# First feed-forward phase of a one-core decoder trunk: the input in four loads, its squares on ScalarE, their sums on VectorE

## Chip, cores and metric

One of the eight cores of a Trainium2 chip runs the whole program. The metric is the time of one execution on the device, in microseconds, as a median over runs. Names of engines in the rows: PE is TensorE (PEld its weight loads), DVE is VectorE, ACT is ScalarE, POOL is GpSimd, SP is the engine that issues most of the loads. A "q" behind a name (SPq, POOLq) is the engine's own instruction queue.

## What is computed

```python
for i in range(DEPTH):                       # DEPTH = 2, so six phases
    h = h + 0.5 * swiglu(rms_norm(h, norm_ff1[i]), ffn1_gate[i], ffn1_up[i], ffn1_down[i])
    hn = rms_norm(h, norm_mix[i])
    ...                                      # i = 0: SSD and RG-LRU mixer, i = 1: differential attention
    h = h + 0.5 * swiglu(rms_norm(h, norm_ff2[i]), ffn2_gate[i], ffn2_up[i], ffn2_down[i])
return rms_norm(h, final_norm)

def rms_norm(x, w, eps=1e-6):
    return x * lax.rsqrt(jnp.mean(x * x, axis=-1, keepdims=True) + eps) * w
def swiglu(x, w_gate, w_up, w_down):
    return (jax.nn.silu(x @ w_gate) * (x @ w_up)) @ w_down
```

x is 256 tokens by 1024 features in float32, and the hidden width is 2816. The work of the change lies wholly in the first `rms_norm` and the first products of the first `swiglu`.

## The kernel before

The residual stream `h` lies in SBUF with features on the partitions: eight tiles of 128 features by 256 tokens. The program goes through six phases: feed-forward (ffn), hybrid mixer (hyb), ffn, ffn, attention (att), ffn. Every matrix is read once from memory in blocks of 128 output columns, 512 KB each (704 KB for the down matrices), into a ring of four slots (`raw`).

**Split products.** To multiply float32 on TensorE, each operand is cut into a high part and the rest. ScalarE copies a block to `whi` (`split_hi`, L168), VectorE subtracts to get `wlo` (`split_lo`, L175). The residual tiles are cut alike into `xn[:, d, 0]` (ScalarE, `residual_hi`, L263, with the norm's weight as scale) and `xn[:, d, 1]` (VectorE, `residual_lo`, L271). `multiply_wide` (L196) then issues two matmuls for each of the eight feature tiles: one of 512 columns (L206) and one of 256 (L207). I call these two a step; a block has eight steps.

**Pairs.** In a ffn phase a gate block and an up block make a pair. There are 22 pairs, then eight pairs of down blocks. Pair 0 is made of blocks 0 and 1, pair 1 of blocks 2 and 3, and so on. Even pairs use PSUM banks 2 and 3, odd ones 0 and 1. So before pair 2 TensorE must know that pair 0 was read out (`s_gu`, L382), which VectorE signals in `merge` (L442).

**The norm.** The factor 1/rms of a token is not applied to x, but to the products: `normalize` (L450) multiplies by `rb`. Here is how `rb` comes about. GpSimd squares the eight tiles and adds them up one by one (`residual_square`, L281; lines 287, 290, 294). TensorE sums over the partitions with a matrix of ones (`token_sums`, L300), ScalarE takes the root (`token_rms`, L314), VectorE the reciprocal (`token_scale`, L320). In every phase the sums stand on TensorE between its first and its second pair (L378).

**Orders.** Every engine runs its own list of instructions in the order in which the functions below issue them. Nothing is scheduled; a wait at the head of a list holds all that stands behind it. SP issues the loads of the start in this order: the vectors `vec`, x tiles 0 to 3, block 0, x tiles 4 to 7, blocks 1, 2, 3, the constants `con`, `heads` (L1595, L1596, L339 to L350). From block 4 on each load waits until its ring slot was split. GpSimd, when it has done the squares of the first phase, clears a part of `arena` and issues the small loads of the hybrid phase (`hyb_weights`, L622) and of `lamin` (L1644).

VectorE's list of the first phase is written in `ffn_vector`, L473 to L485, and ScalarE's in L411 to L420:

```python
for g in range(2):
    before[g]()
    if p0 + g == 0:
        split_lo(dve, 0, 0, DT)
        for d in range(1, DT):
            residual_lo(dve, 0, d)
        split_lo(dve, 1, 1, DT)
    else:
        convert_lo(dve, p0 + g, DT)
token_scale(dve, n)
```

Of the kernel before, what the change touches and what calls it, by code (L numbers as in the profile page):

```python
# [21 lines left out]
D, T, FF = 1024, 256, 2816  # L22
DT, FT = D // P, FF // P
# [50 lines left out]
def trunk(nc, a, out, phases=PHASES):  # L74
    ctx = ExitStack()
    with ctx:
# [35 lines left out]
        s_const = sem("s_const")  # L112
        s_x = [sem(f"s_x{i}") for i in range(2)]
        s_eps = sem("s_eps")
# [8 lines left out]
        s_sq = sem("s_sq")  # L123
        s_acc = sem("s_acc")
        s_stat = sem("s_stat")
        s_rms = sem("s_rms")
# [37 lines left out]
        def load_x(sp, i):  # L164
            tiles = slice(i * DT // 2, (i + 1) * DT // 2)
            sp.dma_start(h[:, tiles, :], a["xT"].rearrange("(d p) t -> p d t", p=P)[:, tiles, :]).then_inc(s_x[i], 16)
# [89 lines left out]
        def fresh(eng, n, d):  # L256

            if n == 0:
                eng.wait_ge(s_x[d // (DT // 2)], 16)
            else:  # L260
                eng.wait_ge(s_h, DT * (n - 1) + d + 1)
# [9 lines left out]
        def residual_lo(dve, n, d):  # L271
            if n == len(phases):
                return
            if n:
# [4 lines left out]
                                     xn[:, d, 0, :].bitcast(F32), ALU.mult, ALU.subtract).then_inc(s_xlo, 1)  # L279

        def residual_square(pool, n, d):  # L281

            fresh(pool, n, d)
            if d == 0:
                if n:
                    pool.wait_ge(s_stat, n)
                pool.tensor_tensor(sumsq[:], h[:, d, :], h[:, d, :], ALU.mult).then_inc(s_acc, 1)  # L287
                return
            pool.wait_ge(s_acc, DT * n + d)
            pool.tensor_tensor(sq[:], h[:, d, :], h[:, d, :], ALU.mult).then_inc(s_sq, 1)  # L290
            if n == len(phases) and d == DT - 1:
                return
            pool.wait_ge(s_sq, (DT - 1) * n + d)
            pool.tensor_tensor(sumsq[:], sumsq[:], sq[:], ALU.add).then_inc(s_acc, 1)
# [5 lines left out]
        def token_sums(pe, n):  # L300

            end = n == len(phases)
            pe.wait_ge(s_acc, DT * (n + 1) - end)
            if n:
                pe.wait_ge(s_rms, n)
            else:
                pe.wait_ge(s_const, 32)
            mm = pe.matmul(sums_bank(n), ones, sumsq[:], start=True, stop=not end)
            if end:
                pe.wait_ge(s_sq, (DT - 1) * (n + 1))  # L310
                mm = pe.matmul(sums_bank(n), ones, sq[:], start=False, stop=True)
            mm.then_inc(s_stat, 1)
# [12 lines left out]
        def add_residual(dve, n, d, acc, scale):  # L325

            dve.wait_ge(s_acc, DT * n + d + 1)
            dve.scalar_tensor_tensor(h[:, d, :], acc, scale, h[:, d, :], ALU.mult, ALU.add).then_inc(s_h, 1)
# [6 lines left out]
        def ffn_sync(sp, n, i):  # L335
# [3 lines left out]
            def gate_up(it, ring_full):  # L339
                for s in range(RING):  # L340
                    if s == 1 and not ring_full:
                        load_x(sp, 1)
                    c = it * (2 * P) + (s // 2) * P
                    load(sp, it * RING + (b0 + s), s,
                         (gate, up)[s % 2][:, bass.ds(c, P)].rearrange("(k p) m -> p k m", p=P), DT, ring_full)
# [13 lines left out]
        def ffn_tensor(pe, n, i):  # L359
# [17 lines left out]
            gate_up(p0, 0, lambda t: pe.wait_ge(s_xlo, DT * n + t + 1), lambda: read_out(pe, p0 - 1))  # L377
            token_sums(pe, n)  # L378
            gate_up(p0 + 1, 1)
            with pe.Fori(1, FT // 2) as it:  # L380
                for g in range(2):
                    pe.wait_ge(s_gu, it * 2 + (hb + g - 1))  # L382
                    gate_up(it * 2 + (p0 + g), g)
# [8 lines left out]
        def ffn_scalar(act, n, i, before):  # L392
# [18 lines left out]
# [3 lines that stand above are left out]
                    split_hi(act, 0, 0, DT, 0)  # L414
                    for d in range(1, DT):
                        residual_hi(act, 0, d)
                    split_hi(act, 1, 1, DT, 0)
                else:
                    convert_hi(act, p0 + g, DT, n > 0)
            token_rms(act, n)  # L420
            for it in range(1, FT // 2):
# [17 lines left out]
        def ffn_vector(dve, n, i, before):  # L439
# [33 lines left out]
            for g in range(2):  # L473
# [6 lines left out]
                else:  # L480
                    convert_lo(dve, p0 + g, DT)
            token_scale(dve, n)
            if n == 0:
# [17 lines left out]
        def down_out(dve, n, d):  # L501
            p = first[n] + FT + d
            dve.wait_ge(s_blk, 2 * p + 2)
            dve.wait_ge(s_acc, DT * n + d + 1)
            acc = wide(0, d % 2)
# [1087 lines left out]
        @block.sync  # L1593
        def _(sp):
            sp.dma_start(vec[:], a["vec"]).then_inc(s_vec, 16)  # L1595
            load_x(sp, 0)  # L1596
            for n, (kind, i) in enumerate(phases):
# [13 lines left out]
        @block.scalar  # L1611
        def _(act):
            act.wait_ge(s_vec, 16)
            act.wait_ge(s_eps, 1)
            before = [lambda: residual_hi(act, 0, 0), lambda: None]
# [21 lines left out]
        def _(pool):  # L1637
            for n in range(len(phases) + 1):
                for d in range(DT):
                    residual_square(pool, n, d)  # L1640
# [69 lines left out]
```

## Time and profile before

| | |
|---|---|
| runs | 1110.90, 1111.77, 1115.74 us |
| median | 1111.77 us |
| span of the profiled execution | 1110.4 us |
| TensorE matmul busy | 1068.7 us, 96% of the span |
| VectorE busy | 827.0 us, 74% |
| ScalarE busy | 600.6 us, 54% |
| GpSimd busy | 169.8 us, 15% |
| read from memory | 184.78 MB, 167 GB/s over the span |

The profiled execution has no time of its own beside its span in what was left; the span lies 1.4 us below the median and 0.5 us below the fastest run. The span is counted from the first instruction to the last. The busy time of matmuls is modelled, so 96% does not say that the engine is at its peak; it says that it is seldom without work.

### The profile page before, as it was taken

Reading aid. Unit: us, or ns where it says so; the run is one execution under the profiler, and the core shown is the slowest. Engines: PE = TensorE matmul, PEld = TensorE weight load, DVE = VectorE, ACT = ScalarE, POOL = GpSimd, SP = SyncE. Lnnn points to the kernel's source line nnn. Section 1 sums busy time; section 2 is a strip of 40 time slices with the busy share of each in tenths; the row PEclk is TensorE's granted clock in tenths of the full one; section 3 lists DMA queues with packets and bytes.
Section 4 is the critical chain, followed back from the end, with each engine's and each line's share of the span. In section 5 each row is a group of like instructions: output and inputs, shape, how many; then the busy total and the mean of one; then the engine's idle time right before and its main releaser. Section 6 shows DMA issues by size and latency. Waiting matters only on the chain.

```text
span 1110.4 us, 18481 instructions
## 1 busy us (share of the span) xinstructions
PE 1068.7 (96%) x6671; PEld 947.7 (85%) x6671; DVE 827.0 (74%) x1150; ACT 600.6 (54%) x915; POOL 169.8 (15%) x156
## 2 busy tenths in 40 slices
PE   6999999999999999999999999999999899999996
PEld 4888888897888998888888888888988888888885
DVE  6878765799887868887656888765679778788753
ACT  5555543565866546555535555544535745555442
POOL 7000011223443330000021000012111041000011
PEclk9999999998998999999999999999999999999999
DMA  8766675454443566667665666676544336666761
GB/s 241 199 193 190 197 208 163 139 145 114 122 115 107 153 181 180 190 195 206 179 191 147 195 191 189 188 205 176 167 137 119 110 92 189 192 191 198 201 187 38
DMA packets 364307, 186.51 MB, mean 168 GB/s; under 512 B 5456, under 2 KB 363984, under 8 KB 364256
## 3 DMA queue, kind: packets, MB, share of 16 engines
q1 hardware_dynamic: 364000, 185.26, 58.9%
q0 software_dynamic: 256, 0.59, 0.2%
q8 instruction: 29, 0.48, 0.2%
q14 instruction: 22, 0.18, 0.0%
HBM read 184.78 MB, written 1.05 MB: 167 GB/s over the span
## 4 chain that ended last, share of the span: by engine, by line
PE 83%; DVE 11%; issue 3%; ACT 2%; POOL 0%; DMA 0%; DVEq 0%; ACTq 0%; SPq 0%; POOLq 0%
PE psum L206 44%; PE psum L207 22%; PE psum L190 5%; PE psum L191 4%; PE psum L192 4%; DVE wlo L178 3%; DVE xn L278 1%; ACT arena L1385 1%; DVE arena L913 1%; DVE small L1490 1%; PE psum L684 1%; DVE arena L1469 0%; PE psum L718 0%; DVE arena L1512 0%; POOL wlo L178 0%
## 5 line engine op out<-in xcount | busy, mean ns | idle before, releaser
L206 PE MATMUL psum<-xn,whi 128*128 128x512 f32 x1408 | 496.2, 397 | 11.2 <-DVE wlo L178 10.3
L178 DVE TENSOR_TENSOR wlo<-raw,whi 128x1024 fp32r<-128x1024 f32 (+1 forms) x317 | 419.4, 1342 | 62.4 <-ACT whi L173 61.5
L207 PE MATMUL psum<-xn,wlo 128*128 128x256 f32 x1408 | 393.9, 280 | 0.0
L173 ACT ACTIVATE whi<-raw 128x1024 fp32r<-128x1024 f32 (+1 forms) x322 | 352.7, 1112 | 46.9 <-PE psum L192 45.1
L206 PEld LDWEIGHTS psum<-xn,whi 128*128 128x128 f32 x1408 | 265.3, 188 | 75.7 <-DVE wlo L178 10.6
L207 PEld LDWEIGHTS psum<-xn,wlo 128*128 128x128 f32 x1408 | 266.7, 189 | 0.1
L206 PE MATMUL psum<-hid,whi 128*128 128x512 f32 x704 | 246.9, 396 | 4.7 <-issue 4.7
L207 PE MATMUL psum<-hid,wlo 128*128 128x256 f32 x704 | 196.9, 280 | 0.0
L206 PEld LDWEIGHTS psum<-hid,whi 128*128 128x128 f32 x704 | 132.0, 188 | 37.1 <-issue 5.9
L190 PE MATMUL psum<-xn,whi 128*128 128x256 f32 x480 | 142.6, 297 | 1.9 <-DVE wlo L178 1.9
L191 PE MATMUL psum<-xn,whi 128*128 128x256 f32 x480 | 138.0, 287 | 0.0
L192 PE MATMUL psum<-xn,wlo 128*128 128x256 f32 x480 | 137.9, 287 | 0.0
L207 PEld LDWEIGHTS psum<-hid,wlo 128*128 128x128 f32 x704 | 132.8, 189 | 0.0
L190 PEld LDWEIGHTS psum<-xn,whi 128*128 128x128 f32 x480 | 94.4, 197 | 6.4 <-issue 5.6
L191 PEld LDWEIGHTS psum<-xn,whi 128*128 128x128 f32 x480 | 94.3, 197 | 1.5 <-issue 1.4
L404 ACT ACTIVATE arena<-arena 128x256 f32<-128x256 f32 x88 | 36.8, 418 | 107.8 <-DVE arena L452 107.8
L192 PEld LDWEIGHTS psum<-xn,wlo 128*128 128x128 f32 x480 | 94.2, 196 | 0.0
L287 POOL TENSOR_TENSOR sumsq<-h 128x256 f32<-128x256 f32 x7 | 5.2, 742 | 578.8 <-DVE h L508 514.8
L269 ACT ACTIVATE xn<-h,vec 128x256 fp32r<-128x256 f32 x48 | 23.3, 505 | 123.0 <-DVE h L508 106.6
L408 ACT ACTIVATE hid<-arena 128x256 fp32r<-128x256 f32 x88 | 36.8, 418 | 88.7 <-DVE arena L457 88.7
L462 DVE TENSOR_TENSOR hid<-arena,hid 128x256 f32 (+1 forms) x88 | 37.4, 425 | 58.5 <-ACT hid L408 58.5
L290 POOL TENSOR_TENSOR sq<-h 128x256 f32<-128x256 f32 x49 | 37.0, 755 | 195.6 <-DVE h L508 172.5
(196 smaller groups left out, 1151.5 us busy)
## 6 DMA issues: line engine op xcount, KB each, us to landing
raw<-in_ffn_gate SPq DMA_DIRECT2D x88, 512.0 KB, 3.8
raw<-in_ffn_up SPq DMA_DIRECT2D x88, 512.0 KB, 4.0
raw<-in_ffn_down SPq DMA_DIRECT2D x64, 704.0 KB, 4.8
raw<-in_hyb_w_in SPq DMA_DIRECT2D x36, 512.0 KB, 3.8
raw<-in_dif_w_qkv SPq DMA_DIRECT2D x24, 512.0 KB, 4.5
raw<-in_hyb_w_out SPq DMA_DIRECT2D x16, 512.0 KB, 4.6
raw<-in_dif_w_o SPq DMA_DIRECT2D x8, 512.0 KB, 4.3
h<-in_xT SPq DMA_DIRECT2D x2, 512.0 KB, 5.4
```

What stands on the lines that cost most here:

```text
L173: act.activation(whi[:, s, 0:k * P], raw[:, s, 0:k * P], ACT.Copy).then_inc(s_whi, 1)
L178: dve.tensor_tensor(wlo[:, s, 0:k * P], raw[:, s, 0:k * P], whi[:, s, 0:k * P].bitcast(F32), ALU.subtract).then_inc(s_wlo, 1)
L190: pe.matmul(acc, w_hi, x[:, t, 0, :], start=start and j == 0, stop=False)
L191: pe.matmul(acc, w_hi, x[:, t, 1, :], start=False, stop=False)
L192: mm = pe.matmul(acc, w_lo, x[:, t, 0, :], start=False, stop=stop and j == k - 1)
L206: pe.matmul(acc, w_hi, x[:, t, :, :], start=start and j == 0, stop=False)
L207: mm = pe.matmul(acc[:, T:2 * T], w_lo, x[:, t, 0, :], start=False, stop=stop and j == k - 1)
L269: act.activation(xn[:, d, 0, :], h[:, d, :], ACT.Copy, scale=vec[:, w:w + 1]).then_inc(s_xhi, 1)
L290: pool.tensor_tensor(sq[:], h[:, d, :], h[:, d, :], ALU.mult).then_inc(s_sq, 1)
L404: act.activation(act_g[:, g, :], gu[:, g, 0, :], ACT.Silu).then_inc(s_silu, 1)
L408: act.activation(hid[:, bass.ds(j, 1), 0, :].rearrange("p a t -> p (a t)"), hu[:, g, :], ACT.Copy).then_inc(s_hhi, 1)
L462: dve.tensor_tensor(v[:, 1, :], hu[:, g, :], v[:, 0, :].bitcast(F32), ALU.subtract).then_inc(s_hlo, 1)
```

## The change

- x comes in four loads of two tiles each, with a semaphore each. The first is issued ahead of `vec`, the second behind it, the third and fourth ahead of blocks 1 and 2.
- ScalarE runs a small Sqrt on `eps` as its first instruction, ahead of its wait for `vec`. Its table load then stands there.
- In the first phase GpSimd does no squares and sums. ScalarE squares the tiles two at a time (`input_squares`), behind its first four weight splits. VectorE adds them up in three halving additions (`input_sums`), behind its first four weight splits and ahead of `token_scale`.
- TensorE's `token_sums` of the first phase stands behind pair 1, not between pairs 0 and 1.
- GpSimd's list begins with `hyb_weights` and the load of `lamin`.
- `down_out` of the first phase no longer waits for GpSimd's sums, and the counts of `s_acc` and `s_sq` are one phase lower.

```diff
         def load_x(sp, i):
-            tiles = slice(i * DT // 2, (i + 1) * DT // 2)
+            tiles = slice(2 * i, 2 * i + 2)
             sp.dma_start(h[:, tiles, :], a["xT"].rearrange("(d p) t -> p d t", p=P)[:, tiles, :]).then_inc(s_x[i], 16)
...
             if n == 0:
-                eng.wait_ge(s_x[d // (DT // 2)], 16)
+                eng.wait_ge(s_x[d // 2], 16)
...
+        xsq = arena[:, 4096:4096 + DT * T].rearrange("p (d t) -> p d t", d=DT)
+
+        def input_squares(act):
+            for d in range(0, DT, 2):
+                act.activation(xsq[:, d:d + 2, :], h[:, d:d + 2, :], ACT.Square).then_inc(s_xsq, 1)
+
+        def input_sums(dve):
+            dve.wait_ge(s_xsq, DT // 2 + 1)
+            dve.tensor_tensor(xsq[:, 0:4, :], xsq[:, 0:4, :], xsq[:, 4:8, :], ALU.add).then_inc(s_xadd, 1)
+            dve.wait_ge(s_xadd, 1)
+            dve.tensor_tensor(xsq[:, 0:2, :], xsq[:, 0:2, :], xsq[:, 2:4, :], ALU.add).then_inc(s_xadd, 1)
+            dve.wait_ge(s_xadd, 2)
+            dve.tensor_tensor(sumsq[:], xsq[:, 0, :], xsq[:, 1, :], ALU.add).then_inc(s_xadd, 1)
...
         def token_sums(pe, n):
...
-            pe.wait_ge(s_acc, DT * (n + 1) - end)
             if n:
+                pe.wait_ge(s_acc, DT * (squares_before(n) + 1) - end)
                 pe.wait_ge(s_rms, n)
             else:
+                pe.wait_ge(s_xadd, 3)
                 pe.wait_ge(s_const, 32)
...
                 for s in range(RING):
-                    if s == 1 and not ring_full:
-                        load_x(sp, 1)
+                    if not ring_full and s in (1, 2):
+                        load_x(sp, s + 1)
...
             gate_up(p0, 0, lambda t: pe.wait_ge(s_xlo, DT * n + t + 1), lambda: read_out(pe, p0 - 1))
-            token_sums(pe, n)
+            if n:
+                token_sums(pe, n)
             gate_up(p0 + 1, 1)
+            if n == 0:
+                token_sums(pe, n)
...
+            if n == 0:
+                input_squares(act)
             token_rms(act, n)
...
+            if n == 0:
+                input_sums(dve)
             token_scale(dve, n)
...
         def _(sp):
+            load_x(sp, 0)
             sp.dma_start(vec[:], a["vec"]).then_inc(s_vec, 16)
-            load_x(sp, 0)
+            load_x(sp, 1)
...
         def _(act):
+            act.wait_ge(s_eps, 1)
+            act.activation(small[:, 0:1], eps[:, 0:1], ACT.Sqrt).then_inc(s_xsq, 1)
             act.wait_ge(s_vec, 16)
-            act.wait_ge(s_eps, 1)
...
             for n in range(len(phases) + 1):
-                for d in range(DT):
+                for d in range(DT) if n else ():
                     residual_square(pool, n, d)
```

The lists of three engines show where things went. TensorE, before, at the end of pair 0 (`sumsq` by `con` is the matmul with ones):

```order
L206 MATMUL psum<-xn,whi 128x512
L207 MATMUL psum<-xn,wlo 128x256
L308 MATMUL psum<-sumsq,con 128x256 [waits s_const,s_acc]
L206 MATMUL psum<-xn,whi 128x512 [waits s_wlo]
L207 MATMUL psum<-xn,wlo 128x256
```

TensorE, changed, at the end of pair 1:

```order
L208 MATMUL psum<-xn,whi 128x512
L209 MATMUL psum<-xn,wlo 128x256
L327 MATMUL psum<-sumsq,con 128x256 [waits s_const,s_xadd]
L402 UNCONDITIONAL_BRANCH
L402 ISA
L202 ISA [waits s_gu]
L208 MATMUL psum<-xn,whi 128x512 [waits s_wlo]
```

The sums moved past the sixteen steps of pair 1, and now stand right ahead of the wait for the read-out of pair 0 (`s_gu`), with which pair 2 begins.

VectorE, changed, from its first weight split on:

```order
L180 TENSOR_TENSOR wlo<-raw,whi 128x1024 [waits s_whi]
L280 SCALAR_TENSOR_TENSOR xn<-h,vec,xn 128x256 [waits s_xhi] x7
L180 TENSOR_TENSOR wlo<-raw,whi 128x1024 [waits s_whi] x3
L291 TENSOR_TENSOR arena<-arena 128x1024 [waits s_xsq]
L293 TENSOR_TENSOR arena<-arena 128x512 [waits s_xadd]
L295 TENSOR_TENSOR sumsq<-arena 128x256 [waits s_xadd]
L341 RECIPROCAL rb<-rms 128x256 [waits s_rms]
L180 TENSOR_TENSOR wlo<-raw,whi 128x1024 [waits s_whi,s_rb]
L472 TENSOR_TENSOR arena<-psum,arena 128x512 [waits s_cor,s_blk]
```

The three additions are new. The reciprocal, the split of block 4 and the read-out of pair 0 (`arena<-psum,arena`, which signals `s_gu`) keep their order behind them.

GpSimd, changed, from its first instruction of the program on:

```order
L651 MEMSET arena 128x2048
L656 DMA arena<-in_lru_w_ra 64x8x64 [waits s_zero]
L656 DMA arena<-in_lru_w_ra 64x8x64
L656 DMA arena<-in_lru_w_ix 64x8x64 x2
L657 DMA arena<-in_hyb_w_in 128x8x16
L1673 DMA small<-in_lam 64x4
```

Before, fifteen squares and additions stood ahead of these rows, the first of them waiting for x; now nothing does.

## Rows read from the trace of the kernel before

**Rows 1.** The page, busy time: engine, us, share of the span, instructions.
```profile
PE 1068.7 (96%) x6671; PEld 947.7 (85%) x6671; DVE 827.0 (74%) x1150; ACT 600.6 (54%) x915; POOL 169.8 (15%) x156
```

**Rows 2.** Chain that ended last, 0 to 28 us: start us, us, what.
```profile
5.14 1.28 ACT L269
6.95 1.07 ACT whi L173
9.27 5.74 DVE xn L278 x7
15.01 1.56 DVE wlo L178
16.61 0.50 PE psum L206
17.92 0.43 PE psum L206
18.35 0.21 PE psum L207
21.23 0.43 PE psum L308 x2
21.66 0.23 PE psum L206
27.21 0.23 PE psum L206
```

**Rows 3.** Timeline of SP: start us, us, queue, line, operation, tile.
```profile
1.68 0.50 SPq L162 DMA_DIRECT2D raw<-in_ffn_gate  x1
2.22 0.58 SPq L166 DMA_DIRECT2D h<-in_xT  x1
```

**Rows 4.** DMA issues at 1.68, 2.22, 2.84, 3.74, 6.21: size, us to landing.
```profile
raw<-in_ffn_gate SPq DMA_DIRECT2D x1, 512.0 KB, 5.3
h<-in_xT SPq DMA_DIRECT2D x1, 512.0 KB, 6.9
raw<-in_ffn_up SPq DMA_DIRECT2D x1, 512.0 KB, 8.1
raw<-in_ffn_gate SPq DMA_DIRECT2D x1, 512.0 KB, 9.0
raw<-in_ffn_up SPq DMA_DIRECT2D x1, 512.0 KB, 8.3
```

**Rows 5.** Stretches: us, busy of PE, PEld, DVE, ACT, POOL, granted clock, DMA share, GB/s.
```profile
5.00:10.00 5.00, 0.68 (x2) 0.50 (x2) 2.46 (x3) 4.84 (x9) 4.29 (x6) 1.00 1.08 311
15.00:20.00 5.00, 4.00 (x13) 3.23 (x14) 4.78 (x4) 1.84 (x2) 4.70 (x4) 0.70 0.62 175
20.00:21.00 1.00, 1.00 (x6) 0.84 (x5) 0.00 (x0) 0.00 (x0) 1.00 (x2) 0.78 0.68 175
```

**Rows 6.** VectorE's cutting of x: one line's durations in ns over the program.
```profile
L278 DVE SCALAR_TENSOR_TENSOR xn<-h,vec,xn x48: 471/485/962, 7.1 to 916.1; 128x256 fp32r<-128x256 f32 x48
```

**Rows 7.** Timeline, 14.9 to 26 us: start us, us, engine, line, operation, tiles.
```profile
14.93 4.86 DVE L178 TENSOR_TENSOR wlo<-raw,whi 128x1024 fp32r<-128x1024 f32 x3
...
23.99 1.23 DVE L178 TENSOR_TENSOR wlo<-raw,whi 128x1024 fp32r<-128x1024 f32 x1
25.13 0.69 DVE L448 TENSOR_TENSOR arena<-psum,arena 128x512 f32<-128x512 f32 x1
...
20.32 1.80 POOL L624 MEMSET arena<- 128x2048 f32 x1
```

**Rows 8.** DMA queues, 22 to 32 us: packets, MB, share of 16 engines.
```profile
q0 software_dynamic: 256, 0.59, 22.1%
```

**Rows 9.** Stretches around a stall of TensorE, columns as in rows 5.
```profile
346.00:348.00 2.00, 0.00 (x0) 0.00 (x0) 2.00 (x2) 0.95 (x1) 1.90 (x1) 1.00 0.54 146
356.00:358.00 2.00, 2.00 (x12) 2.00 (x11) 2.00 (x5) 2.00 (x7) 0.00 (x0) 0.50 0.01 2
```

More of the change, by code:

```diff
@@ L112, in trunk @@
         s_const = sem("s_const")
-        s_x = [sem(f"s_x{i}") for i in range(2)]
+        s_x = [sem(f"s_x{i}") for i in range(4)]
         s_eps = sem("s_eps")
@@ L124, in trunk @@
         s_acc = sem("s_acc")
+        s_xsq = sem("s_xsq")
+        s_xadd = sem("s_xadd")
         s_stat = sem("s_stat")
@@ L279, in residual_lo, with squares_before @@
                                      xn[:, d, 0, :].bitcast(F32), ALU.mult, ALU.subtract).then_inc(s_xlo, 1)
+        xsq = arena[:, 4096:4096 + DT * T].rearrange("p (d t) -> p d t", d=DT)
[9 more added lines that the diff above has]
+            dve.tensor_tensor(sumsq[:], xsq[:, 0, :], xsq[:, 1, :], ALU.add).then_inc(s_xadd, 1)
+        def squares_before(n):
+            return n - 1
         def residual_square(pool, n, d):
@@ L284, in residual_square @@
             if d == 0:
-                if n:
-                    pool.wait_ge(s_stat, n)
+                pool.wait_ge(s_stat, n)
                 pool.tensor_tensor(sumsq[:], h[:, d, :], h[:, d, :], ALU.mult).then_inc(s_acc, 1)
                 return
-            pool.wait_ge(s_acc, DT * n + d)
+            pool.wait_ge(s_acc, DT * squares_before(n) + d)
             pool.tensor_tensor(sq[:], h[:, d, :], h[:, d, :], ALU.mult).then_inc(s_sq, 1)
@@ L292, in residual_square @@
                 return
-            pool.wait_ge(s_sq, (DT - 1) * n + d)
+            pool.wait_ge(s_sq, (DT - 1) * squares_before(n) + d)
             pool.tensor_tensor(sumsq[:], sumsq[:], sq[:], ALU.add).then_inc(s_acc, 1)
@@ L309, in token_sums @@
             if end:
-                pe.wait_ge(s_sq, (DT - 1) * (n + 1))
+                pe.wait_ge(s_sq, (DT - 1) * (squares_before(n) + 1))
                 mm = pe.matmul(sums_bank(n), ones, sq[:], start=False, stop=True)
@@ L325, in add_residual @@
         def add_residual(dve, n, d, acc, scale):
-            dve.wait_ge(s_acc, DT * n + d + 1)
+            dve.wait_ge(s_acc, DT * squares_before(n) + d + 1)
             dve.scalar_tensor_tensor(h[:, d, :], acc, scale, h[:, d, :], ALU.mult, ALU.add).then_inc(s_h, 1)
@@ L503, in down_out @@
             dve.wait_ge(s_blk, 2 * p + 2)
-            dve.wait_ge(s_acc, DT * n + d + 1)
+            if n:
+                dve.wait_ge(s_acc, DT * squares_before(n) + d + 1)
             acc = wide(0, d % 2)
```

## Prediction

> **What bounds the kernel now.** I read the page first. Matmuls keep TensorE busy for 1068.7 of 1110.4 us [rows 1], so a change counts only by what it does to TensorE's line of work. The edits all lie in the first phase, so the next view is the chain of waits of the first 28 us [rows 2]. Until 16.61 us TensorE waits for others; from there on the chain runs on TensorE alone, through pairs 0 and 1 and into pair 2, whose first matmul stands at 27.21. Between 21.66 and 27.21 lie 16 steps, so a step takes 0.347 us at the full clock and a pair 5.55. The granted clock is 0.70 in the mean from 15 to 20 us and 0.78 from 20 to 21 [rows 5]: with two levels, 1 and 0.5, that makes 3.0 and 0.4 us at the lower one (1.2 GHz), 3.4 in all, after a stretch in which TensorE often waited. There a step takes 0.43 + 0.21 = 0.64 us [rows 2]. So a microsecond at the low clock gives away 1 - 0.347/0.64 = 0.46 us.
>
> My measure is the start of pair 2: 27.21 us before. What comes behind it is the same work, on which TensorE is busy without a gap, so the end moves by as much as that start does.
>
> What holds the front? Block 0 is issued at 1.68 and lands 5.3 us later [rows 3, 4], at 6.98, and ScalarE's first split begins at 6.95 [rows 2]. x tiles 4 to 7, issued at 2.22, land at 9.1 [rows 3, 4]. Blocks 1, 2 and 3, issued at 2.84, 3.74 and 6.21, land at 10.9, 12.7 and 14.5 [rows 4], a block each 1.8 us. The DMA share is 1.08 from 5 to 10 us at 311 GB/s [rows 5]: the queue is full. Behind the first weight split VectorE cuts the other seven x tiles in 5.74 us, 0.82 each [rows 2], while the same instruction has a median of 0.485 us over the program [rows 6]. GpSimd is busy 4.29 of those 5 us [rows 5]; I take its squares to be what slows VectorE. The three weight splits behind take 1.62 each [rows 7], against 1.23 for the split at 23.99, when GpSimd does no more squares [rows 7].
>
> **Part 1, x in quarters and the early table load.** The table load of 1.28 us at 5.14 [rows 2] goes to the idle start. It gains nothing: the split behind it needs block 0, which lands at 6.98, and the bytes ahead of block 0 are the same (vec and half of x). The first quarter of x comes earlier, but TensorE needs block 0 beside it. The other table load that goes, ahead of the root, ran while ScalarE was idle: nothing either. The last quarter of x now stands behind block 1. Half of x plus two blocks landed by 9.1 and 10.9, so I put the third quarter at 8.0, block 1 at 10.0, the fourth quarter at 10.9, blocks 2 and 3 as before.
>
> **Part 2, GpSimd leaves.** VectorE's cut is 0.485, its split 1.2. Without any other effect: cuts of tiles 1 to 5 from 9.3 to 11.7, tiles 6 and 7 to 12.7. ScalarE gets to block 1 when it has copied tile 7, at about 11.8, and takes 1.07 [rows 2]; VectorE then splits to 14.1. TensorE could begin block 1 at 14.1 where it began at 16.61: a gain of 2.5 us.
>
> **Part 3, what GpSimd does instead.** Its list now begins with the clearing, 1.80 us [rows 7], so its five loads are issued from about 3 us on, into the full queue. They cost the 16 DMA engines 22.1% of 10 us = 2.2 us [rows 8], for 0.59 MB; at 300 GB/s the bytes alone are 2.0. Lower end: nothing, if they slip in between. Upper end: 2.2 on every landing behind them. I take 2.1 for the fourth quarter and all blocks behind, and 0.9 for block 0 (it lands at 7.9), since the share of 1.08 leaves no room. Then the fourth quarter lands at 13.0; ScalarE copies tiles 6 and 7 to 13.9 and block 1 to 15.0, VectorE splits to 16.2. Block 1 begins at 16.2, a gain of 0.4.
>
> The Trainium skill (DMA: Bandwidth & Descriptors, on queues, rings and completion order) says that each DMA engine takes turns between its queues packet by packet; that speaks against this part, since the later queue gets its turn at once. The same page (anatomy of one DMA) prices the moving at bytes over 436 GB/s, by which the delay would be 1.35 us and the total 0.7 lower; the trace's 22.1% is nearer to the case.
>
> **Part 4, squares and sums.** Four squares of 512 columns on ScalarE, each half a split of 1024 (1.07, so 0.53) [rows 2]: 2.1 us, behind block 3's split. With block 3 landing at 16.6 that is 17.7 to 19.8. On VectorE the additions are 1.2, 0.7 and 0.4 (a read-out of 512 columns is 0.69 [rows 7]): 2.3 us, to 22.1. TensorE does pair 1 until 24.5 or later, so the sums are in time and cost nothing by themselves. Their cover is pair 1.
>
> **Part 5, the sums behind pair 1: the new wait.** Before, from the matmul with ones (21.23 [rows 2]) through the root, the reciprocal and the split of block 4 to the end of the read-out of pair 0 (25.13 + 0.69 = 25.82 [rows 7]) took 4.6 us, and TensorE did pair 1 meanwhile. Now pair 1 is done when this chain begins, and TensorE's next instruction waits for exactly that read-out. The whole 4.6 us, matmul included, lies on TensorE's path. Bounds: none of it is hidden by what stands in the lists, so the lower end is 4.6 less nothing; the upper adds the clock.
>
> **The clock after the stall.** From 346 to 348 us TensorE stood still, and at 356 to 358, busy again, its clock was 0.50 [rows 9]; in the first phase it fell after less idle time than that [rows 5]. So I count a low clock after this stall too: a loss of 3.4 x 0.46 = 1.5 us as in rows 5, or at most that of the 10 us from 348 to 358, 4.6; I take 1.5, since there the wide matmuls of this same phase followed. Below, it is nothing if the clock holds. For pairs 0 and 1 I take the full clock, as the gap ahead of block 1 shrinks to about 1 us between busy work.
>
> **The sum.** Block 1 begins at 16.2; 24 steps of 0.347 are 8.3; slow first steps 0.3; chain 4.6. That gives 29.4 for the start of pair 2, plus 1.5 of clock: 30.9 against 27.2, so 3.7 us more. The span goes to 1110.4 + 3.7 = 1114.1. The span lies 1.4 below the median of the runs, so the median to expect is 1111.8 + 3.7 = **1115.5 us**.
>
> **Rivals.**
> - *The five loads don't delay.* For it: from 22 to 32 us they ran beside block loads, which TensorE did not feel. Against: the queue was not full by then. Block 1 begins at 14.1: 2.1 us less, 1113.4.
> - *The front gain outweighs the stall.* This needs the loads harmless and a clock that stays full after the stall: 14.1 + 8.3 + 4.6 = 27.0, and with no low stretch at all 1111.6; a quicker first block (x is there at 4 us, if block 0 is too) could bring one more, 1110.6. Against it is the clock in rows 9.
> - *Slower by more than 0.5%: the clock falls twice.* The place is pairs 0 and 1 as well as pair 2. If the gap ahead of block 1 costs 3.4 us at the low level as it did before, 1.5 more, and the fall after the stall lasts twice the 3.4 us counted, 1.5 more again: 1115.5 + 3.0 = 1118.5. It decides from about 4 us of low clock beyond those counted (1.8/0.46). For it: the 10 us of rows 9; against: dense wide matmuls follow here.
> - *The change doesn't do what it says:* it was not GpSimd that slowed VectorE. Then the cuts and splits stay at 0.82 and 1.6. The landings hide most of it; the last two cuts and one split add about 1.1: 1116.6.
>
> **Chances.** Forecast 0.45; loads harmless 0.18; gain outweighs 0.12; clock twice 0.17; not GpSimd 0.05; the rest 0.03 for things that I don't see. A measurement of this kernel tells about 0.5%, 5.6 us, from no change. All cases but the clock falling twice lie within that. So slower by more than 0.5% gets 0.17, faster 0.02, within 0.81. The range has to leave out no more than 0.2: it reaches down to 1111.0, into the case of the gain, and up to 1118.8.
>
> **What would show it right or wrong.** In the profile of the changed kernel: the first matmul of pair 2 waits 4 to 5 us for VectorE's read-out (not for a weight split), and its start lies at 29 to 31. GpSimd's loads are issued at 3 to 7 us, and blocks 2 and 3 land at about 14.9 and 16.6; if they land at 12.7 and 14.5, part 3 is wrong. VectorE's seven cuts last 0.5 each; if they last 0.8, part 2 is. The granted clock is 0.50 behind the stall; if it is 1.00 there, 1.5 us go. If pair 2 begins without a gap, part 5 is wrong and the prediction with it; a change of more than 5 us behind 30 us would mean that I looked at the wrong place.

## The result, and the profile after

The kernel with the change takes 1123.97 us (median of 4 runs, 1122.67 to 1126.98), the kernel before 1113.76 beside it (4 runs, 1110.9 to 1117.32). The ratio is 1.0100, with an interval of 1.0073 to 1.0126: about 1% slower. The profiled execution took 1123.17 us, its span is 1121.3, 10.9 more than before. I had forecast 1115.5 and at most 1118.8, so the prediction was wrong. Its direction was right, its size was a third of the real one. The result fell into the case "slower by more than 0.5%", to which I had given 0.17.

The page of the kernel after, busy time per engine, beside [rows 1]:

```profile
PE 1071.6 (96%) x6671; PEld 949.1 (85%) x6671; DVE 827.8 (74%) x1153; ACT 602.4 (54%) x919; POOL 154.3 (14%) x141
```

GpSimd lost 15 us of work, and the others have what they had. So work did not grow much; TensorE waits. The chain of waits of the kernel after, 0 to 40 us (start us, us, what), answers to [rows 2]:

```profile
4.02 11.91 DMA h<-in_xT
15.95 0.91 ACT xn L271 x2
16.86 0.96 ACT whi L175
17.84 1.24 DVE wlo L180
19.12 0.79 PE psum L208
20.13 0.43 PE psum L208
...
22.57 0.23 PE psum L208
29.16 0.45 PE psum L327 x2
29.63 0.48 ACT rms L337
30.14 1.76 DVE rb L341
31.96 1.11 issue
33.07 0.69 DVE arena L472
33.88 0.79 PE psum L208
...
39.37 0.28 PE psum L208
```

Read it in three parts. The front hangs on a DMA: the last quarter of x, issued at 4.02, lands 11.91 us later. (From here on I read a landing off the start of the ScalarE instruction that takes the tiles up, 15.95 here.) Block 1 begins at 19.12, where it began at 16.61. From 29.16 on the chain leaves TensorE: matmul with ones, root, reciprocal, split of block 4, read-out of pair 0 (L472), and only then pair 2, at 33.88. Pair 2 stood at 27.21 before [rows 2]: 6.7 us later. TensorE's waits in the first 50 us (line, what it waited for: us in total, times, longest) give the size of each wait:

```profile
PE psum L208 <- DVE wlo L180: 10.8, 2, 10.4
PE psum L208 <- DVE arena L472: 4.3, 1, 4.3
PE psum L208 <- DVE xn L280: 2.4, 1, 2.4
```

The stretches of the kernel after, columns as in [rows 5]:

```profile
5.00:10.00 5.00, 0.00 (x0) 0.00 (x0) 0.90 (x1) 1.99 (x4) 2.16 (x4) 1.00 1.12 258
10.00:15.00 5.00, 4.21 (x12) 3.22 (x12) 2.31 (x6) 1.07 (x3) 0.00 (x0) 1.00 1.12 195
...
25.00:30.00 5.00, 4.59 (x27) 3.70 (x25) 0.04 (x1) 0.37 (x1) 0.00 (x0) 1.00 0.32 83
30.00:35.00 5.00, 1.11 (x3) 1.02 (x4) 4.79 (x5) 4.18 (x6) 0.00 (x0) 0.75 0.07 20
35.00:40.00 5.00, 5.00 (x19) 4.25 (x19) 3.96 (x7) 2.84 (x5) 0.00 (x0) 0.56 0.69 196
```

From 10 to 15 us the DMA engines are as busy as before (1.12) but move only 195 GB/s. The same stretch of the kernel before:

```profile
10.00:15.00 5.00, 4.75 (x14) 2.67 (x12) 5.00 (x8) 3.50 (x6) 4.33 (x7) 1.00 1.14 322
```

They are busy with something that carries few bytes. From 30 to 35 TensorE works 1.11 us in 5. The granted clock is 0.75 in the mean of that stretch and 0.56 in the next: the lower level of 1.2 GHz until 39.4, where the step drops from 0.64 to 0.35 us (39.37 in the chain). Whose DMA is it? GpSimd's timeline (start us, us, ...) shows its loads now going out from 2.85 us:

```profile
0.74 1.80 POOL L651 MEMSET arena<- 128x2048 f32 x1 [0.29 <-POOLq L1732]
2.85 1.54 POOL L656 DMA_DIRECT2D arena<-in_lru_w_ra  x2 [0.30 <-POOL arena L651]
4.38 1.36 POOL L656 DMA_DIRECT2D arena<-in_lru_w_ix  x2
5.73 0.90 POOL L657 DMA_DIRECT2D arena<-in_hyb_w_in  x1
```

and VectorE's timeline shows that its own part went as hoped:

```profile
10.24 2.06 DVE L280 SCALAR_TENSOR_TENSOR xn<-h,vec,xn 128x256 fp32r<-128x256 f32 x5
16.49 0.88 DVE L280 SCALAR_TENSOR_TENSOR xn<-h,vec,xn 128x256 fp32r<-128x256 f32 x2 [4.19 <-ACT xn L271]
17.84 2.36 DVE L180 TENSOR_TENSOR wlo<-raw,whi 128x1024 fp32r<-128x1024 f32 x2 [0.47 <-ACT whi L175]
...
22.63 1.23 DVE L291 TENSOR_TENSOR arena<-arena 128x1024 f32<-128x1024 f32 x1 [0.86 <-ACT arena L287]
...
30.14 1.75 DVE L341 RECIPROCAL rb<-rms 128x256 f32<-128x256 f32 x1 [5.09 <-ACT rms L337]
```

Five cuts in 2.06 us are 0.41 each, half of the 0.82 before. GpSimd has issued its last load by 7.2 us and does nothing beside them. But 4.19 us stand ahead of the last two, spent waiting for x, and 5.09 ahead of the reciprocal, spent waiting for the matmul with ones.

### The profile page after: what moved, and what is told of

It is laid out like the page before. It is cut to its first block, busy times and chain, and to the rows that moved or that the text cites. A ratio compares the mean times of both kernels' runs of the same rounds, so it can differ in the third digit from the quotient of the medians.

```text
span 1121.3 us, 18460 instructions
## 1 busy us (share of the span) xinstructions
PE 1071.6 (96%) x6671; PEld 949.1 (85%) x6671; DVE 827.8 (74%) x1153; ACT 602.4 (54%) x919; POOL 154.3 (14%) x141
## 4 chain that ended last, share of the span: by engine, by line
PE 81%; DVE 12%; issue 3%; ACT 2%; DMA 1%; SPq 0%; DVEq 0%; ACTq 0%
PE psum L208 44%; PE psum L209 22%; PE psum L192 4%; PE psum L193 4%; PE psum L194 4%; DVE wlo L180 4%; DVE arena L940 2%; DMA h<-in_xT 1%; ACT arena L1412 1%; DVE small L1517 1%; DVE xn L280 1%; DVE arena L1496 0%; DVE rb L341 0%; PE psum L745 0%; PE psum L711 0%
## 5 line engine op out<-in xcount | busy, mean ns | idle before, releaser
L175 ACT ACTIVATE whi<-raw 128x1024 fp32r<-128x1024 f32 (+1 forms) x322 | 352.3, 1112 | 43.8 <-PE psum L194 39.2
L472 DVE TENSOR_TENSOR arena<-psum,arena 128x512 f32<-128x512 f32 x88 | 60.3, 685 | 4.4 <-ACT arena L421 3.9
```

The lines of the kernel that those rows point to most:

```text
L175: act.activation(whi[:, s, 0:k * P], raw[:, s, 0:k * P], ACT.Copy).then_inc(s_whi, 1)
L472: dve.tensor_tensor(gu[:, g, :, :], wide_parts(g)[0], cor[:, g, :, :], ALU.add).then_inc(s_gu, 1)
```

## The experiments

Two things are on trial: GpSimd's small loads in the full queue (front), and the sums behind pair 1 (stall and clock). Each expectation names its own theories A, B and C. The kernel before was run beside each group; its median there was 1113.53, 1114.39 and 1113.18 us (21, 19 and 23 runs, 1107.5 to 1119.8 in all).

**late_small_loads**: the kernel after, GpSimd's loads as late as before.

```diff
+                        pool.wait_ge(s_stat, 1)
                         hyb_weights(pool)
```

> The changed kernel, but GpSimd waits for the first phase's column sums (matmul with ones) before it clears the arena and issues its five small loads. Theory A (the small loads, issued at 2.9 to 6.6 us into a full queue, hold up x's last quarter and block 1): the last quarter, issued at about 4 us, lands near 11 instead of 15.9, block 1 begins near 14 instead of 19.1, pair 2 near 28 to 29 instead of 33.9, and the time falls by 5 to 6 us to about 1118. Theory B (the last quarter is late because it now stands behind block 1 in SP's list, whoever else loads): it lands at 14 or later, pair 2 begins at 32 or later, the time moves by less than 2 us. Both: the wait of 4.3 us at the head of pair 2 stays.

1115.47 us (6 runs), ratio 1.0028 (1.0006 to 1.0049): 8.5 us of median less than the kernel after, from one wait. In the trace the fourth quarter lands at 11.8, where it landed at 15.9. VectorE's timeline of this kernel:

```profile
10.75 2.86 DVE L280 SCALAR_TENSOR_TENSOR xn<-h,vec,xn 128x256 fp32r<-128x256 f32 x7
13.69 2.36 DVE L180 TENSOR_TENSOR wlo<-raw,whi 128x1024 fp32r<-128x1024 f32 x2
```

Seven cuts run through and block 1's split ends at 14.9. The matmul with ones stands at 23.88 (29.16 in the kernel after). The stall is still there in full, on TensorE's timeline:

```profile
28.61 0.79 PE L208 MATMUL psum<-xn,whi 128*128 128x512 f32 x1 [4.30 <-DVE arena L472]
...
29.41 0.63 PE L208 MATMUL psum<-xn,whi 128*128 128x512 f32 x1
30.05 0.63 PE L208 MATMUL psum<-xn,whi 128*128 128x512 f32 x1
```

Steps of 0.64 us behind it show the lower clock, until 31.7. With that clock loss (3.1 us at 0.46) pair 2 stands at 30.0, against 36.4 in the kernel after: 6.4 us come from the small loads.

Block 1 begins at 15.4, not at 14.9 when its split is ready, since TensorE is still at block 0: that block starts at 10.88, and its first steps last 0.64 us. small_loads_after_x, below, has block 1 at 15.4 too.

What the small loads do to the other queue is in the view of the DMA queues from 5 to 15 us (packets, MB, share of 16 engines), first of the kernel after, then of late_small_loads:

```profile
q1 hardware_dynamic: 2832, 1.67, 83.3%
q0 software_dynamic: 256, 0.59, 29.0%
```
```profile
q1 hardware_dynamic: 4929, 3.20, 111.4%
```

GpSimd's queue (q0) takes 2.9 us of the 16 engines' time for itself. SP's queue (q1) moves 1.67 MB in 8.3 us, 200 GB/s, where without the small loads it moves 287: its own packets take 2.5 us longer. Together that is 5.4 us of engine time for 0.59 MB. (The 256 packets of q0 are not the pieces of which I speak below: those, 3072, are counted from the access patterns of the program.)

**sums_between_pairs**: the kernel after, matmul with ones back between pairs 0 and 1.

```diff
-            if n:
-                token_sums(pe, n)
+            token_sums(pe, n)
             gate_up(p0 + 1, 1)
-            if n == 0:
-                token_sums(pe, n)
```

> The changed kernel, but with the matmul with ones back between pair 0 and pair 1. Theory A (its place behind pair 1 costs a stall of 4.6 us): TensorE now waits for the sums instead, from the end of pair 0 at about 22 to 25.1, then does pair 1, and the root, reciprocal and read-out are hidden; pair 2 begins at about 31 instead of 33.9 and the low clock behind it is shorter or gone: 3 to 5 us less, 1119 to 1121. Theory B (the stall only moves; what counts is when the sums are there): pair 2 begins at 33 or later and the time is the same within 1 us.

1116.48 us (10 runs), ratio 1.0037 (1.0018 to 1.0055), 7.5 less than the kernel after. The last quarter still lands at 16, and TensorE waits 1.0 us for the sums, which are ready at 25.1; but pair 2 starts at about 31.4 without a gap, and the clock holds:

```profile
25.00:30.00 5.00, 4.86 (x27) 4.29 (x28) 3.67 (x4) 4.10 (x5) 0.00 (x0) 1.00 0.33 82
30.00:35.00 5.00, 5.00 (x31) 4.35 (x30) 3.96 (x7) 3.22 (x6) 0.00 (x0) 1.00 0.72 202
```

31.4 against 27.2 is 4.2 us, and the ratio says 4.1. Undone alone, each of the two moves gives back 7 to 8.5 us of median; in the traces, start of pair 2 with its clock loss, it is 6.4 (loads) and 5.0 (order) of 9.2. The intervals of the two kernels overlap, so which of the two weighs more is not shown in time. Together they are more than the whole, so with both undone the absence of GpSimd's squares should be a gain (reordered, below, tests it).

**x_quarters_only**: the kernel before, with only x loaded in quarters in the new order.

```diff
...
-            sp.dma_start(vec[:], a["vec"]).then_inc(s_vec, 16)
             load_x(sp, 0)
+            sp.dma_start(vec[:], a["vec"]).then_inc(s_vec, 16)
+            load_x(sp, 1)
```

> The kernel before with nothing but the loads of x in quarters, in the order of the change (first quarter ahead of the vectors, last behind block 1). GpSimd still squares. Theory A (the order alone costs little): block 1 begins within 1 us of 16.6, pair 2 within 1 us of 27.2, the same time as before within 2 us. Theory B (the last quarter's place is costly): block 1 begins at 18 or later, pair 2 at 29 or later, 2 us or more slower.

1113.09 us (10 runs), ratio 0.9999 (0.9981 to 1.0016). The last quarter lands at 10.84, and block 1 begins at 17.3, 0.7 later than before; GpSimd still slows VectorE:

```profile
9.87 5.71 DVE L278 SCALAR_TENSOR_TENSOR xn<-h,vec,xn 128x256 fp32r<-128x256 f32 x7
15.50 4.02 DVE L178 TENSOR_TENSOR wlo<-raw,whi 128x1024 fp32r<-128x1024 f32 x3
```

0.82 a cut, as in [rows 2], with GpSimd's squares in place: it is they, and not the loads of x, that slow VectorE. The order of x costs nothing and brings nothing by itself in time.

**large_pieces**: late_small_loads plus the same bytes (0.59 MB) through GpSimd's queue at 1.28 us, but in pieces of 4608 bytes.

```diff
+                        pool.dma_start(arena[:, 7168:7168 + NCON], a["con"]).then_inc(s_big, 16)
                         pool.wait_ge(s_stat, 1)
+                        pool.wait_ge(s_big, 16)
                         hyb_weights(pool)
```

> As late_small_loads, but GpSimd issues at its very start one load of the same 0.59 MB in large pieces (4608 bytes each, the constants once more, into the part of the arena that is cleared later). Theory A (the count of small pieces of 64 and 256 bytes costs, not the bytes): the last quarter of x lands within 2.1 us of the kernel with late small loads, so at 13 or sooner, and pair 2 begins at most 2 us after it. Theory B (any 0.59 MB there costs the 5 us): it lands at 15 or later and pair 2 begins at 33 or later.

1113.5 us (one run, span 1111.7). Block 0 lands at 9.6, 1.1 later than without, the last quarter at 13.0, 1.2 later, the matmul with ones is at 25.54, 1.7 later. The same bytes in 2048 pieces of 256 bytes and 1024 of 64 made the last quarter 4.1 later. So it is not the bytes alone. Two things differ besides the size of the pieces, and no run parts them. The large load goes out at 1.28 us, 1.6 us ahead of the first small one; yet from 5 to 15 us this kernel moves 328 and 307 GB/s, the kernel after 258 and 195 at about the same share, so no such load is hidden there. And it is one load to 128 partitions, where the 256-byte pieces come in four loads to 64 partitions each.

**early_256_only and early_64_only**: the kernel after, with only one kind of small piece early. The first puts the wait ahead of the 64-byte load:

```diff
+            pool.wait_ge(s_stat, 1)
             pool.dma_start(wdt, a["hyb_w_in"][0][:, COL_DT:COL_DT + HEADS].rearrange("(k p) m -> p k m", p=P)
```

The second issues that load first, at 1.27 us, and waits ahead of everything else.

> The changed kernel, but of the five small loads only the four in pieces of 256 bytes (2048 pieces, 0.52 MB) are issued early; the one in pieces of 64 bytes and the last tiny one come behind the sums. Late small loads had the last quarter of x at 11.8, all early at 15.9. Theory A (cost by bytes): 0.52 of 0.59 MB, it lands at 15.5. Theory B (cost by pieces, 2048 of 3072): 14.5. Theory C (the 64-byte pieces are the dear ones): 13 or sooner.

> The changed kernel, but only the load in pieces of 64 bytes (1024 pieces, 0.07 MB) is issued early, as GpSimd's first instruction, the clearing and all others behind the sums. Theory A (bytes): the last quarter of x lands at 12.3 at most. Theory B (pieces, 1024 of 3072): about 13.2. Theory C (the 64-byte pieces are the dear ones): 14 or later.

With the four 256-byte loads early (1123.63 us, one run) the last quarter lands at 15.2: 3.4 of the 4.1 us are theirs. With the 64-byte load alone, early, it lands at 11.3: no delay. Both are nearest to theory A, the cost by bytes (15.5, and 12.3 at most), not to the count of pieces (14.5 and 13.2). So between the two kinds of small pieces their number does not set the cost. SP's timeline shows a second trace of it. The issue of the constants takes 5.70 us in the kernel after, 4.75 with the 256-byte loads early, and 2.23 in late_small_loads (each row from its own kernel: after, early_256_only, late_small_loads):

```profile
10.18 5.70 SPq L368 DMA_DIRECT2D con<-in_con  x1
```
```profile
10.35 4.75 SPq L368 DMA_DIRECT2D con<-in_con  x1
```
```profile
9.50 2.23 SPq L368 DMA_DIRECT2D con<-in_con  x1
```

The time of early_64_only was not foreseen: 1123.97 us, span 1122.2, as slow as the kernel after, although its first 40 us are those of late_small_loads (sums at 24.08). Where those 10 us lie is told in the last section.

**small_loads_after_x**: the kernel after, the loads only once x is in (`pool.wait_ge(s_x[3], 16)` ahead of them).

> The changed kernel, but GpSimd waits for the last quarter of x before it clears and issues its small loads, so they come at about 14 us. Theory A: the last quarter lands near 11.8 and block 1 begins near 14.9 as with loads behind the sums; only blocks 3 and 4 and the constants, still in the queue then, land later, and pair 2 begins within 1 us of 28.5. Theory B (the loads cost the same wherever in the first 20 us they come): pair 2 begins at 31 or later.

1111.72 us (one run, span 1109.9). The last quarter lands at 11.4, the matmul with ones is at 23.87, pair 2 at 28.60 behind the stall of 4.3. GpSimd clears from 11.4 us on and issues from 13.5 to 17.8. The same pieces there, beside the end of block 3, the constants and the blocks from 4 on, delay nothing that TensorE waits for. The rate falls here too: 241 and 196 GB/s from 15 to 20 and 20 to 25 us, at shares of 1.12 and 1.17.

**old_small_loads_first**: the kernel before, with its small loads ahead of its squares on GpSimd's list.

```diff
+            if any(kind == "hyb" for kind, _ in phases):
+                hyb_weights(pool)
+            pool.dma_start(lamin, a["lam"]).then_inc(s_lamin, 16)
             for n in range(len(phases) + 1):
...
-                if n == 0:
-                    if any(kind == "hyb" for kind, _ in phases):
-                        hyb_weights(pool)
-                    pool.dma_start(lamin, a["lam"]).then_inc(s_lamin, 16)
```

> The kernel before with GpSimd's clearing and five small loads ahead of its squares instead of behind them; all else as before. Theory A (small loads into a full queue hold up whatever is queued behind): x tiles 4 to 7, issued at 2.2, land at 12 or later instead of 9.1, block 1 begins at 19 or later instead of 16.6, pair 2 at 29.5 or later instead of 27.2; 2 to 5 us slower. Theory B (it took the quarters' order as well): block 1 begins within 1 us of 16.6 and the time is the same within 1.5 us.

1116.89 us (9 runs), ratio 1.0022 (1.0004 to 1.0040). Half a miss: I expected x tiles 4 to 7 at 12 or later and block 1 at 19 or later; they landed at 9.5, and it began at 17.07. Block 1's transfer did take 11.8 us instead of 8.1 [rows 4], 3.7 more:

```profile
raw<-in_ffn_up SPq DMA_DIRECT2D x1, 512.0 KB, 11.8
```

But here all of x is issued ahead of block 1 and came in time, and VectorE would not have reached block 1 much earlier anyhow. The delay costs so much in the changed kernel because the last quarter of x stands behind block 1, and VectorE no longer hides it. TensorE also waits 1.3 us for the sums, which GpSimd begins at 7.26, 2.1 us later than before.

**readout_first and late_readout_first**: the kernel after, and late_small_loads, with the split of block 4 and the read-out of pair 0 ahead of root and reciprocal (ScalarE's list alike).

```diff
...
+                split_lo(dve, 4, 0, DT)
+                merge(0, 0, 0, True)
+                token_scale(dve, 0)
+                normalize(0, 0)
+                split_lo(dve, 5, 1, DT)
...
```

> The changed kernel with only VectorE's and ScalarE's order altered: the split of block 4 and the read-out of pair 0 stand ahead of root and reciprocal. The small loads stay early. Theory A (TensorE stalls for the read-out, which stood behind the reciprocal): the read-out ends before pair 1 does, so pair 2 begins at about 29.7 instead of 33.9 without the 4.3 us wait and at the full clock; then the second block of pair 2 or pair 3 waits 1 to 3 us for weights split behind the reciprocal; in all 4 to 6 us less than the changed kernel. Theory B (the chain through root and reciprocal is needed anyway and only shifts by one pair): pair 3 waits over 4 us, and the time falls by less than 2.

> Both single edits on the changed kernel: small loads behind the sums, and read-out of pair 0 ahead of root and reciprocal. Theory A (each wait is of its own and they add up): pair 2 begins near 24.5 without a wait, its second block waits about 1.5 us for weights split behind the reciprocal, pair 3 waits under 1.5 us for the read-out of pair 1 and begins near 32 instead of 35; the clock stays full; the time is about 3 us below that of late small loads, near 1112. Theory B (as the alteration of the order alone seemed to say, nothing is won): the time is that of late small loads, 1115 to 1116.

1123.87 us (4 runs), ratio 1.0071 (1.0043 to 1.0099), and 1115.54 us (10 runs), ratio 1.0019 (0.9998 to 1.0040). The trace of the first shows the stall of 4.3 us broken up (TensorE's timeline, the waits in brackets):

```profile
34.76 0.50 PE L208 MATMUL psum<-xn,whi 128*128 128x512 f32 x1 [1.44 <-DVE wlo L180]
...
38.45 0.49 PE L208 MATMUL psum<-xn,whi 128*128 128x512 f32 x1 [0.59 <-DVE arena L475]
```

Pair 3 begins at 38.45, where it begins at 42.03 in the kernel after. In late_readout_first pair 3 begins at 33.03, in late_small_loads at 35.6. The mechanism is there, but the intervals overlap with those of the kernels without it: in time this edit alone is not shown, and my forecasts of 4 to 6 us and of 1112 were misses. In the two profiled executions the loss is traced: behind 60 us readout_first had the longer of TensorE's two steps, 0.353 instead of 0.347 us, for 4.6 us more than the kernel after (last section), and 4.6 less 3.6 is the 1.0 by which its span is longer.

**reordered**: late_small_loads, with squares 0 and 1 ahead of the first weight split on ScalarE, 2 and 3 ahead of the fourth, the additions ahead of the fourth split on VectorE, the matmul with ones between the two blocks of pair 1, and the read-out first as above.

```diff
+                    input_squares(act, (0, 2))
                     split_hi(act, 0, 0, DT, 0)
...
+                    split_hi(act, 2, 2, DT, 0)
+                    input_squares(act, (4, 6))
+                    split_hi(act, 3, 3, DT, 0)
...
+            gate_up(p0 + 1, 1, before_up=(lambda: None) if n else (lambda: token_sums(pe, n)))
```

> A kernel built from what the first four runs showed: the changed kernel with (1) GpSimd's small loads behind the first phase's column sums, (2) two of the four squares ahead of ScalarE's first split, where it waits for block 0, and two ahead of its fourth, VectorE's three additions ahead of its fourth split, (3) the matmul with ones between the two blocks of pair 1, (4) the split of block 4 and the read-out of pair 0 ahead of root and reciprocal. Theory A (the stall is the order of root, reciprocal and read-out, and the front gain is real once the small loads are gone): block 1 begins near 15, pair 2 near 24 without a wait of over 0.5 us and at the full clock, 3 to 4 us ahead of the kernel before; the time is 3 to 4 us less than its, about 1110. Theory B (the runs' scatter of 5 us or other places swallow it): pair 2 is early, but the time is within 1.5 us of the kernel before. If pair 2 begins behind 26 us, my reading of the waits is wrong.

1110.28 us (9 runs) against 1114.39, ratio 0.9960 (0.9946 to 0.9974): faster than both kernels, by about 4.5 us against before. TensorE waits once, at the start, and never again in the first 50 us:

```profile
PE psum L208 <- DVE wlo L180: 11.2, 1, 11.2
```
```profile
20.00:25.00 5.00, 5.00 (x30) 4.38 (x29) 3.71 (x4) 2.71 (x3) 2.40 (x2) 1.00 0.90 256
25.00:30.00 5.00, 5.00 (x31) 4.35 (x30) 3.98 (x6) 3.22 (x5) 3.71 (x6) 1.00 0.70 189
```

The matmul with ones stands at 21.80, with 8 steps of 0.347 of pair 1 to come, so pair 2 begins at about 25.0: 2.2 us before the 27.21 of [rows 2]. That is 1.0 later than I expected, as block 1 begins at 16.1 and not near 15. The interval of the ratio is 2.9 to 6.0 us; why it is more than 2.2 was not settled.

**reordered_x_first**: the same with both later quarters of x ahead of block 1.

```diff
-                    if not ring_full and s in (1, 2):
-                        load_x(sp, s + 1)
+                    if not ring_full and s == 1:
+                        load_x(sp, 2)
+                        load_x(sp, 3)
```

> The reordered kernel with the third and the fourth quarter of x both ahead of block 1, so that only blocks stand behind. Theory A (the last quarter of x ends the wait for block 1's split): ScalarE copies the last tiles about 1 us earlier, block 1 begins near 14 instead of 14.9, pair 2 up to 1 us earlier than in the reordered kernel; the time is at least as good, about 0.5% below the kernel before. Theory B (block 1 then lands later itself, behind 0.26 MB more): block 1 begins at 14.5 or later and nothing is gained.

1111.75 us (12 runs) against 1113.18, ratio 0.9992 (0.9969 to 1.0015): no gain over reordered can be told, and by its own interval none over before either. In its trace block 1 begins at 15.0 and the matmul with ones is at 20.81, 1.0 earlier than in reordered, and the profiled span of 1105.3 is the lowest of all. But block 0, which both orders load at the same place, landed at 8.2 instead of 8.8, so the order of x is not shown to be the reason. Single runs reach from 1106.6 to 1117.1.

## Why the prediction was wrong, step by step

The measure was the start of pair 2 with its clock loss: forecast 29.4 + 1.5 = 30.9, found 33.88 + 2.5 = 36.4, before 27.2.

- **Parts 1 and 4 held, part 2 in its mechanism.** Block 0 lands at 8.0 (forecast 7.9). Cuts of 0.41 (forecast 0.485) and splits of 1.2 us, beside 0.82 in x_quarters_only, show that GpSimd's squares had slowed VectorE. Squares (2.17) and additions (2.35) end at 25.1, 3 us later than forecast but ahead of the end of pair 1 at 29.2.
- **Part 2 left out TensorE's own work on block 0.** "TensorE could begin block 1 at 14.1": with the loads out of the way it begins at 15.4 (late_small_loads, small_loads_after_x), as the steps of block 0 take 0.64 us at first. The gain that was to be had was 1.2 us, not 2.5: **+1.3**.
- **Part 3 was mis-sized, and this is the step that failed most.** "I take 2.1 for the fourth quarter": it was 4.1 against late_small_loads, and the last quarter landed at 15.9, not 13.0; blocks 2 and 3 landed at 17.7 and 19.4, not 14.9 and 16.6. I priced the loads by the share of the DMA engines' time that they took for themselves, 2.2 us [rows 8], and took that as the upper end. It was none: in the full queue they took 2.9 for themselves, and SP's packets beside them took 2.5 longer. The second part could have been read off the trace of before, in the same view as [rows 8]:

```profile
q1 hardware_dynamic: 3246, 1.63, 67.0%
```

That is 243 GB/s for SP's queue beside the small loads, against 285 from 5 to 15 us without them. 0.59 MB in one load of large pieces cost 1.2 us, and 0.52 MB in 2048 pieces of 256 bytes cost 3.4. For the large pieces bytes over 436 GB/s is a fair price (the Trainium skill, DMA: Bandwidth & Descriptors, anatomy of one DMA): the estimate by it is 1.35 us, and large_pieces shows 1.2. For the small pieces the same estimate is far off. I also weighed it against this part that the later queue gets its turn at once. That was the wrong way round: the turns are taken from the earlier queue, and the last quarter, issued ahead of three of the five loads, was held up all the same. Block 1 began 3.7 us later than without the loads, forecast 2.1: **+1.6**, and with the 1.3 above it stood at 19.1 instead of 16.2.
- **The clock of pairs 0 and 1.** I took it as full, because I expected a short gap. With x late TensorE waited 2.4 us in the middle of block 0, and the steps from 19.12 to 22.4 last 0.64 us. The 24 steps took 10.0 us, forecast 8.6: **+1.4**. This was the place of my slower rival, and it is a consequence of part 3: in late_small_loads block 1 follows without a gap, and its 24 steps take 8.5 us.
- **Part 5 held**: from the matmul with ones to pair 2 4.7 us, forecast 4.6; every kernel that keeps this order shows the wait of 4.3.
- **The clock after the stall** was low for 5.5 us of work, from 33.9 to 39.4, forecast 3.4: 2.5 us lost, not 1.5: **+1.0**. In late_small_loads it was 3.1 us.

With 0.1 in the chain that makes 5.4 us more, 9.1 to 9.2 in place of 3.7. The traces hold it to the end: the matmuls with ones, which close each phase, stand at 207.82 before and 215.67 after (+7.9), 414.58 and 423.12 (+8.5), 601.53 and 611.35 (+9.8), 920.48 and 930.26 (+9.8), and the ends are 10.9 apart. The changes by about 1.2 us in feed-forward phases are no work of the change; the last section says what they are. The 0.7 us within the hybrid phase was not traced.

The range failed with part 3: its upper end held the low clock twice, but no case in which the small loads cost more than their own share. The case that came true, over 0.5% slower, came true for a reason of its own: of the 5.4 us, 2.4 are low clock, 1.6 the loads and 1.3 block 0. The rival that the loads don't delay was wrong, and the one that the front gain outweighs the stall would be right only with the front of late_small_loads and the order of reordered.

## What to carry to other kernels

A load that gets its turn earlier takes the turn from something: before moving small loads forward, ask which transfer then lands last. Price them in a full queue from a stretch or a run in which pieces of that size went beside other loads, and count how much slower the other queue's bytes went there, not only the share that the small loads took. When work is taken from an engine that only disturbed others, the order around it has to be set anew too; here most of the same edits were 1% slower in one order and 0.4% faster in another. A sum that must be known before the next stage belongs ahead of the last work that can cover its chain.

## What was not expected of the hardware

**TensorE's step has two lengths at the full clock.** Groups of TensorE's instructions, 60 to 120 us (line, names, shapes, count | busy us, mean ns), of the kernel after and of early_64_only, both with a granted clock of 1.00:

```profile
L208 PE MATMUL psum<-xn,whi 128*128 128x512 f32 x174 | 60.4, 394 | 0.0
L209 PE MATMUL psum<-xn,wlo 128*128 128x256 f32 x174 | 48.2, 277 | 0.0
```
```profile
L208 PE MATMUL psum<-xn,whi 128*128 128x512 f32 x171 | 60.5, 399 | 0.0
L209 PE MATMUL psum<-xn,wlo 128*128 128x256 f32 x170 | 47.7, 281 | 0.0
```

60.4 us over 174 steps are 0.347 each, 60.5 over 171 are 0.354. A step of one wide and one narrow matmul takes 0.347 or 0.353 us in the mean of every loop sampled, never between, and the same along a whole loop as far as I sampled it. A gate and up loop has 352 steps (2.3 us between the levels), a down loop 176 (1.2 us); with four such phases the ends can differ by up to 14 us. early_64_only was at the long step in all eight loops, late_small_loads in three of them: three loops of 2.3 and two of 1.2 make about 9.2 of the 10.6 us between their spans; most of the rest arises within the hybrid phase and was not traced. Between the kernels before and after it is one loop of 1.2 less and two of 1.2 more, the steps of the differences above. Within one trace loops of the same instructions have both levels (the gate and up loops of the kernel before: 0.347, 0.353, 0.347, 0.347). Each kernel has one trace, so whether a loop of a given kernel always has the same level is open, and so is how much of the small differences in time above is due to it. That this is also the scatter of the times (1107.5 to 1119.8 us for the kernel before) fits in size but was not traced run by run, and what sets the level was not tried.

**The granted clock in the records starts late.** From 19.1 to 22.4 us of the kernel after the column says 1.00, while the steps last 0.64 us, as they do at a granted clock of 0.50 behind the stall. Until TensorE's matmuls first reached their short durations the column stayed at 1.00 in the traces that I compared; where they had reached them and fell back, the column shows it (0.70 from 15 to 20 us before [rows 5], 0.77 in early_256_only, 0.75 in readout_first). At the start the durations of the matmuls tell the clock, and the column does not.

**The price of small pieces.** 2048 pieces of 256 bytes held up the other queue's transfers by 3.4 us where 0.59 MB in pieces of 4608 bytes took 1.2, and 1024 pieces of 64 bytes, issued at 1.27 us ahead of most others, cost nothing that could be seen. Whether those would cost in the full queue is open: only the remaining 0.7 us of the 4.1 could be theirs. That the size of the pieces does it, and not the four loads to 64 partitions, was not tested.
